# Loading an expert's down weights as one transfer of 4 KB rows instead of two of 2 KB rows

## What is computed

```python
weights = softmax(e_top) * g_prob                       # top-1 group of 4, then top-2 of its 4 experts
combine = sum_k weights[n, k] * one_hot(expert[n, k], 16)
hg = einsum('nd,edf->nef', x, w_gate)                   # w_gate, w_up: 16 x 1024 x 512
hu = einsum('nd,edf->nef', x, w_up)
act = silu(hg) * hu * combine[:, :, None]
y = einsum('nef,efd->nd', act, w_down)                  # w_down: 16 x 512 x 1024
```

## Time and profile before

| | |
|---|---|
| times of three runs | 1343.43, 1345.60, 1347.21 us (median 1345.6) |
| the profiled execution | 1345.38 us, of it the span 1343.7 us |
| PE busy | 1251.2 us, 93% of the span |
| DVE, ACT, POOL busy | 50%, 40%, 16% |
| mean granted TensorE clock | 0.968 of full speed |
| expert loop | from about 1010 to 1307 us of the span |

### The profile page before, as it was taken

One profiled execution on the slowest core, in us unless ns is written; L12 is line 12 of the kernel. 1 busy time (PEld: TensorE's weight loads), 2 busy tenths in 40 slices (PEclk: granted clock), 3 DMA queues, 4 the chain that ended last, 5 costly groups with the idle time before them and its releaser, 6 DMA issues. The chain is left out here.

```text
span 1343.7 us, 17997 instructions
## 1 busy us (share of the span) xinstructions
PE 1251.2 (93%) x7171; PEld 945.4 (70%) x7171; DVE 666.9 (50%) x918; ACT 536.4 (40%) x867; POOL 208.6 (16%) x235
## 2 busy tenths in 40 slices
PE   3699999999999999999879999999989999999997
PEld 0477787776778887887755667647757888877762
DVE  0625533221251215022366552154687889888877
ACT  2333223101173117214433332212346777777742
POOL 2420400020000001001200002100025322222220
PEclk8699999999999999999789999999989999999988
DMA  9452311253441535536679997812289999999972
GB/s 364 175 204 64 102 63 63 94 166 126 165 181 60 182 133 218 164 128 256 238 255 357 355 352 228 275 54 102 79 304 307 337 375 374 377 373 374 369 278 95
DMA packets 126347, 294.48 MB, mean 219 GB/s; under 512 B 10152, under 2 KB 10272, under 8 KB 121608
## 3 DMA queue, kind: packets, MB, share of 16 engines
q1 hardware_dynamic: 107608, 241.21, 51.0%
q0 software_dynamic: 18672, 52.32, 10.9%
HBM read 270.43 MB, written 30.42 MB: 224 GB/s over the span
## 5 line engine op out<-in xcount | busy, mean ns | idle before, releaser
L981 PE MATMUL psum<-part,part 128*128 128x512 f32 (+1 forms) x1088 | 444.1, 408 | 6.3 <-DVE part L2301 3.6
L983 PE MATMUL psum<-part,part 128*128 128x512 f32 (+1 forms) x1088 | 430.1, 395 | 0.0
L982 PE MATMUL psum<-part,part 128*128 128x512 f32 (+1 forms) x1088 | 430.0, 395 | 0.0
L981 PEld LDWEIGHTS psum<-part,part 128*128 128x128 f32 (+1 forms) x1088 | 228.0, 210 | 71.3 <-issue 24.5
L983 PEld LDWEIGHTS psum<-part,part 128*128 128x128 f32 (+1 forms) x1088 | 227.7, 209 | 40.2
L982 PEld LDWEIGHTS psum<-part,part 128*128 128x128 f32 (+1 forms) x1088 | 228.8, 210 | 36.0
L2301 DVE TENSOR_TENSOR part<-arena,part 128x2048 fp32r<-128x2048 f32 x96 | 217.5, 2289 | 33.7 <-ACT part L1746 32.3
L1845 DVE TENSOR_TENSOR part<-arena,part 128x2048 fp32r<-128x2048 f32 x42 | 96.4, 2300 | 244.5 <-PE psum L1023 220.1
L1746 ACT ACTIVATE part<-arena 128x2048 fp32r<-128x2048 f32 x94 | 177.8, 1918 | 36.1 <-DMA arena<-in_w_up_dram 20.4
L1521 ACT ACTIVATE arena<-psum 128x512 f32<-128x512 f32 (+4 forms) x142 | 77.2, 570 | 250.4 <-PE psum L983 198.9
L969 PE MATMUL psum<-cst,arena 128*128 128x128 f32 (+3 forms) x857 | 123.5, 285 | 49.9 <-DMA cst<-in_consts_dram 12.4
(11 more groups left out here) (282 smaller groups left out, 1118.7 us busy)
## 6 DMA issues: line engine op xcount, KB each, us to landing
arena<-in_w_in_dram SPq DMA_DIRECT2D x34, 1024.0 KB, 5.5
arena<-in_cache_kv_w_dram SPq DMA_DIRECT2D x16, 2048.0 KB, 11.6
arena<-in_w_gate_dram SPq DMA_DIRECT2D x32, 1024.0 KB, 9.2
arena<-in_w_up_dram SPq DMA_DIRECT2D x32, 1024.0 KB, 8.8
arena<-in_w_down_dram SPq DMA_DIRECT2D x32, 1024.0 KB, 10.0
arena<-in_w_ada_dram SPq DMA_DIRECT2D x24, 1024.0 KB, 7.5
arena<-in_cache_kv_w_dram SPq DMA_DIRECT2D x16, 1024.0 KB, 9.4
arena<-in_w_ada_final_dram SPq DMA_DIRECT2D x8, 1024.0 KB, 8.1
```

Source lines behind the costliest of these rows:

```text
L981: nc.tensor.matmul(out_, hi, w_hi, start=start, stop=False)
L982: nc.tensor.matmul(out_, hi, w_lo, start=False, stop=False)
L983: last_product[0] = nc.tensor.matmul(out_, lo, w_hi, start=False, stop=stop)
```

## The change

`expert_half` gives down halves 4 and 5 other room: the whole raw matrix stands in one slot (`down_raw`, 4 rows of 1024 floats in each partition), the high part of both in the next; a half is then the left or the right 512 columns of each of the four pieces. The load of the down matrix is one transfer of 2 MB whose rows are 4 KB, on one semaphore (`half_in[4]`). It is issued when both halves of the room have been read (`y0_filled` and `y1_filled`), and `high(4)` and `high(5)` both wait for it. The split is still made half by half, and nothing changes in the arithmetic, in the order on PE, ACT and DVE, or in the loads of up and gate.

```diff
+        down_raw = shaped(nc.alloc_sbuf_tensor_at("down_raw", [P, 4 * D], F32, offset=base + 4 * (4 * SLOT))[:, :], (4, D))
+
         def expert_half(n):
             first = n * SLOT
-            return at(first, 4, CH), *parts(first + HALF, first, 4, CH)
+            if n < 4:
+                return at(first, 4, CH), *parts(first + HALF, first, 4, CH)
+            return tuple(a[:, :, (n - 4) * CH:(n - 3) * CH] for a in (
+                down_raw, *parts(5 * SLOT, 4 * SLOT, 4, D)))
...
             def load(w, e, at_, h):
-                src = w[bass.ds(e, 1)] if at_ < 4 else w[bass.ds(e, 1), :, h * CH:(h + 1) * CH]
-                src = src.rearrange("a (k p) n -> p (a k) n", p=P)
-                src = src[:, 4 * h:4 * h + 4, :] if at_ < 4 else src
-                sp.dma_start(expert_half(at_ + h)[0], src).then_inc(half_in[at_ + h], 16)
+                src = w[bass.ds(e, 1)].rearrange("a (k p) n -> p (a k) n", p=P)
+                sp.dma_start(expert_half(at_ + h)[0], src[:, 4 * h:4 * h + 4, :]).then_inc(half_in[at_ + h], 16)
+
+            def load_down(e):
+                src = t["w_down"][0][bass.ds(e, 1)].rearrange("a (k p) n -> p (a k) n", p=P)
+                sp.dma_start(down_raw, src).then_inc(half_in[4], 16)
+
+            def next_down(n, e):
+                for read in (y0_filled, y1_filled):
+                    sp.wait_ge(read, n)
+                load_down(e)
...
-            for h in range(2):
-                load(t["w_down"][0], 0, 4, h)
+            load_down(0)
...
-                    next_pair(t["w_down"][0], 4, DOWN_READ, n + 2, one)
+                    next_down(n + 2, one)
             next_pair(t["w_up"][0], 2, UP_READ, rounds * E_ALL, E_ALL - 1)
-            next_pair(t["w_down"][0], 4, DOWN_READ, rounds * E_ALL, E_ALL - 1)
+            next_down(rounds * E_ALL, E_ALL - 1)
...
-            pool.wait_ge(half_in[5], rounds * (E_ALL * 16))
+            pool.wait_ge(half_in[4], rounds * (E_ALL * 16))
...
-                act.wait_ge(half_in[at_], loads)
+                act.wait_ge(half_in[min(at_, 4)], loads)
```

More of the change, by code:

```diff
@@ L740, in _ @@
             load_modulation(sp, 1)
-            GATE_READ, UP_READ, DOWN_READ = (gate_read, gate_filled), (up_read, up_filled), (y0_filled, y1_filled)
+            GATE_READ, UP_READ = (gate_read, gate_filled), (up_read, up_filled)
             rounds = rounds_of(sp)
```

## The result

The changed kernel takes 1369.1 us (median of 4 runs, 1364.8 to 1377.9) against 1345.2 us: a ratio of 1.019, 95% interval 1.013 to 1.024. It is slower, by some 24 us. The profiled execution took 1366.8 us, its span is 1365.1 us, 21.4 us more than the span before.

A forecast was written before the change was run, and what follows sets the result against it. Prediction: PE (18.01 us per expert) bounds the early experts, the DMA queue (18.55) the late ones; the change makes a serial chain of L + 10.8 us. 1345.4 + 11.2 + 4.5 = 1361 us, 8-in-10 range 1349 to 1380.

The forecast's parts named there:

- L: Time from issue to landing of the 2 MB down load in the expert loop; forecast 8.4 us, between 7.6 and 8.9.
- Two paces: Expert loop before the change: early experts run at PE's 18.01 us, late ones at the DMA queue's 18.55 us.
- The 1.35 us for a scatter: DMA queue: a gather or scatter of POOL falling between two 1 MB loads adds 1.35 us to the 2.65.
- The chain, L + 10.8 us: Down load issue, landing, high part, low part, hidden_low, down products, next issue: an expert can't be shorter than this sum.
- No leftover of the backlog: Queue at the down load's issue: gate loads already out, so earlier loads add 0 to L; backlog rival 12.6 us, chance 0.02.
- L = 8.4: Chosen landing time: 7.6 us from w_pa's 2 MB load, plus up to 1.3 for the scatter beside the down load.
- The sum over 13 experts: Experts 1 to 14: 19.2 us each against 18.34, +11.2 us in all (+0.8 to +17.7).
- L = 8.9: Upper case, scatter paid in full beside the down load: 1345.4 + 17.7 + 5.6 = 1369 us.
- L = 7.6: Lower case, scatter passes before the down load's data: 1345.4 + 0.8 + 3.3 = 1349.5 us.
- The clock: Rival: half clock behind PE's waits in every second expert, +11 us on 1369, 1380; chance 0.12 including a longer L.
- The end: Expert 15, without next gate work to cover its load: +4.1 us later down products, 0.4 more for them, +4.5.
- The rival "hidden": Down load lands within 7.2 us, wait hidden, whole rows gain: 1344 to 1346 us; chance 0.11 including loads of 7.2 to 7.6.

The follow-up runs named there:

- experiment 6: POOL's scatter writes only 16 result rows of an expert: in the changed kernel 1357.4 us, ratio 1.011; in the kernel before 1337.7 us, ratio 0.9955.
- experiment 9: Kernel before with the down matrix cut into upper and lower 256 rows, 1 MB halves of whole 4 KB rows, products reordered: 1339.3 us, ratio 0.9970.
- experiment 10: Kernel before with down matrix cut into upper and lower rows, products reordered, each half loaded as two 0.5 MB transfers of 2 KB rows: 1342.0 us, ratio 0.9993.
- experiment 7: Changed kernel with two more products per expert into a bank nobody reads, ahead of PE's wait for the down weights: 1371.7 us, ratio 1.020.
- experiment 5: Changed kernel with a further 0.5 MB load, into room nobody reads, issued just ahead of each expert's down load: 1411.1 us, ratio 1.051.
- experiment 8: Changed kernel with a further 0.5 MB load ahead of each down load, plus four unread products per expert during PE's wait: 1398.6 us, ratio 1.041.

## Why the prediction was right, point by point

It forecast slower, 1361 us in a range of 1349 to 1380; measured were 1369.1. The closed chain, on which all rests, was right. Two of its terms came out near the measured numbers partly by luck, as the points on the backlog and on L say.

- **Two paces.** Right and shown: 18.01 us is PE's, 18.55 the queue's (experiments 6, 9 and 10). The 1.35 us for a scatter, read from one gap between two landings, was right as well (1.3 between experiments 7 and 6).
- **The chain, L + 10.8 us.** Right. The expert shown above took 8.7 + 11.0; the chain after the landing is 0.15 us longer than the sum of its rows. Experiment 5 lengthened L and the expert with it.
- **No leftover of the backlog.** The term of 0 did little harm, but its reason was wrong. L is 7.8 to 9.9 us and not 12.6, and the DMA share is under 1. But the gate loads were to take 5.5 to 7.5 us and to be out of the queue before the next down load. They take about 9, presumably because the up loads ahead of them wait for the 2 MB of down weights. The second gate load of an expert, issued at 1203.90, is one of them:

```profile
arena<-in_w_gate_dram SPq DMA_DIRECT2D x1, 1024.0 KB, 9.6
```

  It landed at 1213.46, 2.5 us after the next down load was issued (1210.99). For experts 8 to 14 this is 1.5 to 3.5 us. Where it is 3.4 or 3.5 the down load takes 8.5 to 8.9 us (issues at 1191.33, 1229.71, 1268.08), where it is 2.5 or 2.6 it takes 7.8 to 7.9 (1210.99, 1249.23). So in the late half the queue still reaches into L.
- **L = 8.4.** A little low: the mean of the 13 loads is 8.75 us. That it is so near is partly luck, for the term on top of 7.6 was to be the scatter, 1.1 us after the tokens and so right beside the load. In the changed kernel the scatter isn't there. Early in the loop it starts ahead of the down load or long after it: in one expert 9.9 us after its issue, when it has landed (1119.93 against 1110.02 and 1119.12). For experts 8 to 14 it starts 2.8 to 4.4 us after the issue, and lands after the load. What makes L long early is by all signs the gather. It starts 1.1 us ahead of the down load (1108.92 against 1110.02) and lands beside it, at 1118.54; there L is 8.9 to 9.9, and experiment 6 leaves these loads nearly as long. Later the gather starts 4.9 us ahead (1206.10 against 1210.99), and L is 7.8 to 8.9. No run moves the gather alone.
- **The sum over 13 experts.** Forecast +11.2, measured +20.9. It is made up of 13 x 0.35 = 4.6 for L, 13 x 0.15 = 2.0 for the chain, and two stretches at half clock, 1.7 us each: 11.2 + 4.6 + 2.0 + 3.4 = 21.2. (The prediction's sum for L = 8.9 adds 5.6 us for the end where its own terms, 4.6 and 0.4, give 5.0, and that for L = 7.6 leaves out the 0.4. Both move its corners by under 1 us.)
- **The clock** was the rival that came true in part. In the changed kernel the two stretches begin at 1062.7 and 1144.6, at the end of PE's waits of 2.1 and 2.6 us, and the experts that hold them took 22.0 and 22.2 us, where their neighbours took 20:

```profile
1062.70:1066.10 3.40, 3.40 (x10) 2.66 (x9) 3.40 (x2) 2.91 (x3) 0.66 (x2) 0.50 1.05 387
1144.60:1148.00 3.40, 2.93 (x7) 2.38 (x8) 3.40 (x3) 3.40 (x3) 0.00 (x0) 0.50 1.05 395
```

  That it costs time behind a wait is shown by experiment 8, in a kernel with longer waits; in the changed kernel itself it is read from the profile.
- **The end.** Forecast +4.5, measured +4.2: the last down load was issued at 1307.04 and took 9.1 us, and its products began at 1321.20. That is 14.2 us after the copy of expert 14, against 9.3 before: +4.9, where 4.1 were forecast. From there to the last copy it took 7.8 us against 8.4, where 0.4 more were forecast, so two small errors cancel.
- **The rival "hidden"** fell: no load landed within 7.2 us. The gain that it rested on is real, though. Whole rows save 0.33 us of queue for an expert (experiments 9 and 10); no run shows that the changed kernel had anything of it, as its queue was full no longer (a DMA share of 0.92 and 0.98).

## What to carry to other kernels

A transfer into a single set of room closes a loop: read, issue, land, prepare, read. Sum that loop before merging two transfers, because the merged one starts at the later of two releases and is usable at the later of two landings. One at a time the two delays hide behind one another (+4 and +13 us), together they don't (+41, of which some 17 are the clock that falls behind the longer waits). A forecast of such a loop also needs the place in time of the other traffic: the down loads took 9.1 to 9.5 us with the full scatter 1.5 us behind them (experiment 7) and 7.8 to 8.9 with it some 4 us behind (the late half of the changed kernel).

If longer rows are what is wanted, cut the matrix the other way, so that a half consists of whole rows, and reorder the products instead of joining the waits.

When one resource is relieved, look for the bound that stands next: here the queue's 0.3 us were worth having only in the kernel whose queue was still full.

## What was unexpected of the hardware

- Products that nobody reads made a kernel 12.5 us faster (1411.1 to 1398.6, ratios 1.051 and 1.041), by keeping the granted clock at 1.00 in place of 0.87 to 0.91 through a wait of nearly 4 us in each expert.
- The clock fell to 0.5 already behind waits of PE of 2.1 and 2.6 us, in 2 of 13 experts of the changed kernel.
- With POOL's full scatter issued 1.5 us behind it, a load of 2 MB on SP took 9.3 us, with a scatter of 16 rows at the same place 8.0.
- One 2 MB load of 4 KB rows took 8.75 us in the loop on average; two 1 MB loads of 2 KB rows, issued 0.6 us apart at the same place, had both landed 9.2 us after the first issue.
- A 128 x 2048 split in four strided pieces of 512 takes the same time on DVE as a contiguous one, 2290 against 2292 ns.
